# Causal attention on latent heads: score, transposition and weighted-sum products in a new order over eight PSUM banks

## The reference, cut to what matters

```python
q = (_rmsnorm(cq, q_norm) @ w_uq).reshape(B, S, H, MLA_NOPE + MLA_ROPE)
kv = (_rmsnorm(ckv, kv_norm) @ w_ukv).reshape(B, S, H, MLA_NOPE + MLA_V)
...
k = jnp.concatenate([kv[..., :MLA_NOPE], k_rope], axis=-1)
v = kv[..., MLA_NOPE:]
o = _dense_causal_attention(q * (MLA_NOPE + MLA_ROPE) ** -0.5, k, v)
return o @ w_out
```

## Time and profile before

| what | value |
|---|---|
| median of three runs | 4548.55 us (4546.48 to 4549.56) |
| the profiled execution | 4549.86 us |
| its span in the profile | 4548.1 us |
| TensorE busy, whole span | 94% |
| the mla stage, first score to first product of mla_out | 2483.86 to 2652.44 us |
| granted TensorE clock, mean of the stage | 0.86 of full |

### The profile page before, as it was taken

The page is one execution under the profiler, slowest core; times in us unless marked ns, Lnnn a source line. Parts: engine busy times, 40 slices in busy tenths (PEclk is TensorE's granted clock), DMA queues, the critical chain, the costliest instruction groups (busy, mean ns, idle before and its releaser), DMA issues.

```text
span 4548.1 us, 40760 instructions
## 1 busy us (share of the span) xinstructions
PE 4278.2 (94%) x15992; PEld 2741.9 (60%) x15992; DVE 1575.2 (35%) x2912; ACT 685.8 (15%) x1462; POOL 1670.0 (37%) x1520
## 2 busy tenths in 40 slices
PE   7948999999999999999999789999999889989998
PEld 3324444444644444488863348888888436847887
DVE  3062111026711110333225633324432754453432
ACT  1131000012610000100012420001000231211000
POOL 0002988800049887044410004443444015003442
PEclk9969999999899999899999889999999889989999
DMA  3103434321034342122221012222222123102222
GB/s 122 65 0 111 157 143 157 117 72 56 10 134 157 143 157 102 60 88 88 86 71 43 1 47 88 88 86 77 88 81 90 52 80 99 36 28 84 84 88 70
DMA packets 124350, 387.45 MB, mean 85 GB/s; under 512 B 37568, under 2 KB 40640, under 8 KB 110080
## 3 DMA queue, kind: packets, MB, share of 16 engines
q1 hardware_dynamic: 108848, 302.56, 20.0%
q0 software_dynamic: 15312, 82.28, 4.7%
HBM read 376.40 MB, written 8.39 MB: 85 GB/s over the span
## 4 chain that ended last, share of the span: by engine, by line
PE 90%; DVE 6%; ACT 2%; issue 1%; DMA 0%; POOL 0%; DVEq 0%; POOLq 0%; ACTq 0%
PE bank L723 89%; ACT temporary L1340 1%; DVE temporary L2370 1%; DVE small_columns L2158 1%; DVE temporary L2155 1%; ACT normed L1340 0%; ACT area_b L1340 0%; DVE normed L1740 0%; DMA vector_columns<-in_vectors_dram 0%; DVE temporary L1898 0%; DVE area_b L1861 0%; DVE temporary L1974 0%; DVE small_columns L1978 0%; DVE temporary L1902 0%; PE bank L1002 0%
## 5 line engine op out<-in xcount | busy, mean ns | idle before, releaser
L723 PE MATMUL bank<-normed,weight_ring 128*128 128x512 f32 (+2 forms) x4080 | 1508.9, 527 | 17.4 <-DVE normed L1746 5.8
L723 PEld LDWEIGHTS bank<-normed,weight_ring 128*128 128x128 f32 (+1 forms) x4080 | 779.6, 192 | 698.1 <-issue 636.8
L723 PE MATMUL bank<-area_a,weight_ring 128*128 128x512 f32 (+1 forms) x1776 | 636.4, 515 | 8.2 <-issue 8.2
L723 PEld LDWEIGHTS bank<-area_a,weight_ring 128*128 128x128 f32 x1776 | 339.3, 192 | 282.0 <-issue 259.7
L723 PE MATMUL bank<-area_b,weight_ring 128*128 128x256 f32 (+3 forms) x1616 | 501.9, 458 | 5.8 <-issue 2.8
L673 POOL TENSOR_TENSOR area_b<-weight_ring 128x512 f32<-128x512 f32 (+1 forms) x68 | 84.2, 1239 | 1141.3 <-issue 569.7
L643 POOL TENSOR_SCALAR area_b<-area_b,small_columns 128x384 f32<-128x384 f32 x336 | 417.8, 1243 | 0.0
L723 PEld LDWEIGHTS bank<-area_b,weight_ring 128*128 128x128 f32 (+2 forms) x1616 | 303.7, 188 | 179.7 <-issue 148.7
L645 POOL TENSOR_TENSOR area_b<-area_b 128x384 f32<-128x384 f32 x336 | 334.4, 995 | 28.0
L723 PE MATMUL bank<-area_b 128*128 128x256 f32 (+2 forms) x1200 | 258.6, 378 | 16.2 <-ACT area_d L1340 16.2
L673 POOL TENSOR_TENSOR area_d<-weight_ring 128x512 f32<-128x512 f32 (+1 forms) x68 | 84.2, 1239 | 446.6 <-PE bank L723 422.2
(11 more groups left out here) (277 smaller groups left out, 4535.8 us busy)
## 6 DMA issues: line engine op xcount, KB each, us to landing
weight_ring<-in_weights_dram SPq DMA_DIRECT2D x377, 512.0 KB, 4.6
weight_ring<-in_weights_dram SPq DMA_DIRECT2D x61, 1024.0 KB, 4.8
area_b<-in_weights_dram POOLq DMA_DIRECT2D x48, 1024.0 KB, 5.4
area_b<-in_weights_dram POOLq DMA_DIRECT2D x48, 512.0 KB, 6.6
weight_ring<-in_weights_dram SPq DMA_DIRECT2D x40, 384.0 KB, 4.3
weight_ring<-in_weights_dram SPq DMA_DIRECT2D x24, 256.0 KB, 3.8
low_scratch<-area_d SPq DMA_DIRECT2D x16, 256.0 KB, 2.0
area_d<-low_scratch SPq DMA_DIRECT2D x16, 256.0 KB, 2.8
```

The lines of the kernel that those rows point to most:

```text
L723: i = pe.matmul(out, lhsT, rhs, start=start, stop=stop)
```

## The change

Only the stage "mla" changes; the number of units, heads and blocks stays.

1. **Banks.** Scores get banks 4 to 7 by unit, turned blocks banks 0 and 1 by unit, outputs banks 2 and 3 by head. The table `MLA_ORDER` goes; each kind of result has its own semaphores.
2. **Outputs one block at a time.** The four output products of a head are no longer issued together. Product b of head hd is issued in the turn of unit 4·hd + b + 8 (`MLA_OUT = 8`), between that unit's score and the turned blocks of the unit three before. Each head's first one waits until ACT has copied the head's four units.
3. **Scale and mask.** DVE adds the mask only to the unit's own 128 columns (the diagonal block), in place in the bank, and takes the maximum straight from the bank. The scale goes into the exponential (`scale=`) and into the negation of the maximum. ACT's exponential reads the bank and writes `TM`.
4. **1/sum.** DVE no longer multiplies the probabilities by 1/sum. It writes a 128x128 diagonal matrix of 1/sum (`ts(mla_diagonal(v), const("ident"), ...)`), four of them in turn in the last row of `D` ("area_d").
5. **Transposition as a product.** In place of a transposition TensorE does a float32 product of the unnormalised block with the diagonal matrix, which transposes and normalises at once: two passes of 128 columns in place of one.
6. **ACT's order.** exp(u), then (every fourth unit, from the third head on) the store of the head three behind, then copy(u-2).

```diff
-stage("mla", 0, 16 * 9, 0)
+stage("mla", 0, 0, 0)
...
+        MLAG, MLA_OUT = 3, 8
+
+        def mla_scores(u):
+            return bank[4 + u % 4]
+
+        def mla_diagonal(u):
+            return D[:, 9, u % 4 * P:(u % 4 + 1) * P]
+
+        def mla_turned(u):
+            return bank[u % 2]
+
+        def mla_output(hd):
+            return bank[2 + hd % 2]
...
-            for u in range(16 * NB + MLAG):
+            for u in range(16 * NB + MLA_OUT):
                 if u < 16 * NB:
                     hd, n = u // NB, u % NB
-                    s = small()
-                    mm(sbank(s)[:, 0:(n + 1) * P], A[0:96, hd, n * P:(n + 1) * P], B[0:96, hd, 0:(n + 1) * P], True, True,
-                       small_full)
-                if u >= MLAG:
+                    if u >= 4:
+                        pe.wait_ge(S("mla_exp"), u - 3)
+                    mm(mla_scores(u)[:, 0:(n + 1) * P], A[0:96, hd, n * P:(n + 1) * P], B[0:96, hd, 0:(n + 1) * P],
+                       True, True, S("mla_scored"))
+                if u >= MLA_OUT:
+                    hd, b = (u - MLA_OUT) // NB, (u - MLA_OUT) % NB
+                    if b == 0:
+                        pe.wait_ge(S("mla_copied"), NB * hd + NB)
+                        if hd >= 2:
+                            pe.wait_ge(S("mla_stored"), hd - 1)
+                    rows = slice(64 * (hd % 2), 64 * (hd % 2) + 64)
+                    mm(mla_output(hd)[rows, b * P:], A[:, 16 + 2 * b + hd // 8, hd % 8 * 64:hd % 8 * 64 + 64],
+                       B[:, 16 + 4 * (hd % 2) + b, b * P:], b == 0, b == NB - 1,
+                       S("mla_summed") if b == NB - 1 else None)
+                if 0 <= u - MLAG < 16 * NB:
                     v = u - MLAG
-                    hd, n = v // NB, v % NB
-                    s = small()
+                    n = v % NB
                     pe.wait_ge(S("mla_probs"), v + 1)
+                    if v >= 2:
+                        pe.wait_ge(S("mla_copied"), v - 1)
                     for b in range(n + 1):
-                        i = pe.transpose(sbank(s)[:, b * P:(b + 1) * P], TM[:, v % 4, b * P:(b + 1) * P], const("ident"))
-                    i.then_inc(small_full, 1)
-                    if n == NB - 1:
-                        o = small()
...
+                        mm(mla_turned(v)[:, b * P:(b + 1) * P], TM[:, v % 4, b * P:(b + 1) * P], mla_diagonal(v), True, True,
+                           S("mla_transposed") if b == n else None)
...
-                    p = TM[:, o, 0:(n + 1) * P]
-                    a(p, p, ACT.Exp, bias=SM[:, o:o + 1], accum_out=SM[:, 4 + o:5 + o]).then_inc(S("mla_exp"), 1)
...
+                    a(TM[:, o, 0:(n + 1) * P], mla_scores(u)[:, 0:(n + 1) * P], ACT.Exp, scale=scale, bias=SM[:, o:o + 1],
+                      accum_out=SM[:, 4 + o:5 + o]).then_inc(S("mla_exp"), 1)
...
-                    stook(stt(w, sbank(s)[:, 0:(n + 1) * P], scale, C[:, CAT["causal"] + 512 - (n + 1) * P:CAT["causal"] + 512],
-                              ALU.mult, ALU.add), s)
-                    sdone(dve, s)
+                    w, own_keys = mla_scores(u)[:, 0:(n + 1) * P], mla_scores(u)[:, n * P:(n + 1) * P]
+                    dve.wait_ge(S("mla_scored"), u + 1)
+                    own(tt(own_keys, own_keys, C[:, CAT["causal"] + 384:CAT["causal"] + 512], ALU.add))
                     own(dve.tensor_reduce(SM[:, o:o + 1], w, AX, ALU.max))
...
-                    ts(w, w, SM[:, 8 + o:9 + o], None, ALU.mult).then_inc(S("mla_probs"), 1)
+                    if v >= 4:
+                        dve.wait_ge(S("mla_transposed"), v - 3)
+                    ts(mla_diagonal(v), const("ident"), SM[:, 8 + o:9 + o], None, ALU.mult).then_inc(S("mla_probs"), 1)
```

More of the change, by code:

```diff
@@ L1094, in _ @@
             begin("mla_out")
-            sdone(pe, mla_small("output", 14))
-            sdone(pe, mla_small("output", 15))
+            pe.wait_ge(S("mla_stored"), 16)
             for j in range(DB):
@@ L1574, in _, with stored @@
                 took(a(B[0:64, j, :], pbank(m0 + j)[0:64, :], ACT.Identity), m0 + j)
-            for u in range(16 * NB + MLAG - 1):
+            scale = float(96 ** -0.5)
+            def stored(hd):
+                rows = slice(64 * (hd % 2), 64 * (hd % 2) + 64)
+                act.wait_ge(S("mla_summed"), hd + 1)
+                a(H[rows, hd // 2, :], mla_output(hd)[rows, :], ACT.Identity).then_inc(S("mla_stored"), 1)
+            for u in range(16 * NB + MLA_OUT):
                 if u < 16 * NB:
@@ L1577, in _ @@
                     n, o = u % NB, u % 4
+                    if u >= 4:
+                        act.wait_ge(S("mla_transposed"), u - 3)
                     act.wait_ge(S("mla_minus_max"), u + 1)
[L1579 to L1582 removed]
+                    a(TM[:, o, 0:(n + 1) * P], mla_scores(u)[:, 0:(n + 1) * P], ACT.Exp, scale=scale, bias=SM[:, o:o + 1],
+                      accum_out=SM[:, 4 + o:5 + o]).then_inc(S("mla_exp"), 1)
@@ L1583, in _ @@
+                if u >= MLA_OUT + NB and u % NB == 0:
+                    stored(u // NB - 3)
                 v = u - MLAG + 1
-                hd, n = v // NB, v % NB
-                s = mla_small("turned", v)
-                sfull(act, s)
-                if v >= 8 and n == 0:
-                    sfull(act, mla_small("output", hd - 2))
-                stook(a(B[:, 16 + 4 * (hd % 2):17 + 4 * (hd % 2) + n, n * P:(n + 1) * P],
-                        sbank(s)[:, 0:(n + 1) * P].rearrange("p (b t) -> p b t", t=P), ACT.Identity), s)
@@ L1591, in _ @@
-                if n == NB - 1:
-                    s = mla_small("output", hd)
-                    rows = slice(64 * (hd % 2), 64 * (hd % 2) + 64)
-                    sfull(act, s)
-                    stook(a(H[rows, hd // 2, :], sbank(s)[rows, :], ACT.Identity), s)
+                if 0 <= v < 16 * NB:
+                    hd, n = v // NB, v % NB
+                    act.wait_ge(S("mla_transposed"), v + 1)
+                    if v >= 8 and n == 0:
+                        act.wait_ge(S("mla_summed"), hd - 1)
+                    a(B[:, 16 + 4 * (hd % 2):17 + 4 * (hd % 2) + n, n * P:(n + 1) * P],
+                      mla_turned(v)[:, 0:(n + 1) * P].rearrange("p (b t) -> p b t", t=P), ACT.Identity)\
+                        .then_inc(S("mla_copied"), 1)
@@ L1596, in _ @@
+            stored(15)
             norm(8)
@@ L2150, in _ @@
                     n, o = u % NB, u % 4
[L2151 to L2157 removed]
+                    w, own_keys = mla_scores(u)[:, 0:(n + 1) * P], mla_scores(u)[:, n * P:(n + 1) * P]
+                    dve.wait_ge(S("mla_scored"), u + 1)
+                    own(tt(own_keys, own_keys, C[:, CAT["causal"] + 384:CAT["causal"] + 512], ALU.add))
                     own(dve.tensor_reduce(SM[:, o:o + 1], w, AX, ALU.max))
[L2159 removed]
+                    ts(SM[:, o:o + 1], SM[:, o:o + 1], -scale, None, ALU.mult).then_inc(S("mla_minus_max"), 1)
                 if u >= 1:
```

19 lines of the change are left out of this document (removed).

## The result

| | before | after |
|---|---|---|
| median | 4548.74 us (4 runs) | 4508.38 us (4505.63 to 4512.0, 4 runs) |
| profiled execution | 4549.86 us | 4505.63 us |
| span | 4548.1 us | 4503.8 us |
| stage, first score to first product of mla_out | 168.6 us | 128.5 us |
| one head in the steady state, clock at 1.00 | 9.09 us | 7.91 us |

The ratio is 0.9913, with a 95% interval of 0.9895 to 0.9930: 40 us faster, where 54.8 were forecast. The stage is 40.1 us shorter, and that is all of the median's difference. At full clock 16 heads give 16·(9.09 − 7.91) = 18.9 us of it; the other 21.2 is time that the kernel before spent at the lower clock, less a difference at the ends. The profiled execution is 4 us better still: its stage starts 2.9 us earlier than before, behind the same instructions.

A forecast was written before the change was run, and what follows sets the result against it. Before, DVE's work and the output products between a score and its user set the head's length; after, TensorE bounds it: 16·6.9 + 3.4 = 113.8 us against 168.6, 54.8 less, so 4494 us, range 4484 to 4515.

The forecast's parts named there:

- A: Stage mla: the clock keeps falling, mean 0.86, a head takes 8.0 us and the kernel 4512 us; chance 15%.
- B: Stage mla: ACT's strict order stalls TensorE once a head, 1.2 us, 19 us in all, kernel 4513 us; chance 8%.
- TensorE's waits behind the output products go: Stage mla: DVE's wait of 2.60 us a head loses its cause; TensorE's own waits are small and at the ends.
- TensorE becomes the bound: Stage mla: TensorE at 6.9 us a head exceeds DVE's 5.3 and ACT's 4.7, so it sets the pace.
- DVE's total, 5.3 us a head: DVE in stage mla: 6.49 us less 0.81 for scale and mask and 0.40 for normalisation, at most 5.7.
- The clock: Stage mla: mean granted clock 0.97 or more after the change, against 0.86 before.
- C: Stage mla: the clock falls to 0.50 and stays, a head takes 13.8 us, kernel slower at 4604 us; chance 4%.
- The diagonal product, 1.3 us a head dearer: TensorE in stage mla: 2.54 us a head for diagonal products against 1.2 for transpositions, 21 us in all.
- TensorE's total, 6.9 us a head: TensorE in stage mla: scores 2.14, outputs 2.14, diagonal products 2.54 and 0.1 more, at full clock.
- A diagonal pass, 0.127 us: TensorE's turned blocks: each pass takes 0.127 us, from eight such passes in 1.16 us; 20 passes a head.
- The ends, 3.4 us: Start and end of stage mla: 1.9 us lost in the first eight units, 0.65 for the last copy, 0.85 for the store.
- The cause: Stage mla: spreading the output products, at most one before a score in its unit, removes DVE's 2.60 us wait a head.

## Why the prediction was right, and where it was off

Time, sign and range held: 4508 within 4484 to 4515, but 14 us above the 4494 of the forecast, so a quarter of the forecast gain was missing. The forecast's own band (a head between 6.6 and 7.4 us, 4489 to 4502) was missed. That 4508 lies in the range at all is luck: the range reached up to 4515 to take in the rivals A (4512) and B (4513), neither of which occurred; what came in their place was a cost of 1.36 us a head that the prediction had at 0.1.

- *TensorE's waits behind the output products go.* Right, by the waits.
- *TensorE becomes the bound.* Right: 99% occupied, 1.6 us of waits.
- *DVE's total, 5.3 us a head.* Right: 73.8 of 110 us, 5.3 of 7.91. So it was nowhere near deciding.
- *The clock.* Right: 1.00, and with it the 20 us that the forecast gave to the lower clock less the ends (21.2 measured); of the 35 us for the head at full clock only 18.9 came. Rivals A and C didn't occur, nor B: TensorE waited for ACT 0.3 us in all.
- *The diagonal product, 1.3 us a head dearer.* Right in size (7.91 − 6.60 = 1.31), by the run that undid it, but with luck: ten passes are 1.1 of it, and 0.2 is the dearer step back from 64 columns, which the prediction didn't know. Its passes at 0.127 in place of 0.11 made up for that.
- *TensorE's total, 6.9 us a head.* **This step failed**, at the term "0.1 because ten passes that should take 7·0.43 + 0.27 = 3.28 took 3.39 to 3.41". That 0.11 to 0.13 was read from a piece in which only one group followed another, output products and then a score; it is the price of one step from 64 to 128 columns (the same piece takes 3.25 with 128 columns throughout), and I entered it as one for the head. The changed order has four steps to 64 and four back. Measured: 6.55 without them, and 1.36 for them. The 6.9 held 0.35 too much, nearly all of it the diagonal passes (20·(0.127 − 0.11) = 0.34), and lacked the 1.36: 6.9 − 0.35 + 1.36 = 7.91.
- *A diagonal pass, 0.127 us.* Measured: 0.11. The group of eight that it was read from the earlier trace rows stands right behind passes with 64 columns. A little earlier in the same trace the same kind of group stands behind passes with 128 columns and takes 1.05 us, not 1.16. The 0.11 between them is what the turned blocks lose here too (0.33 against 0.22); the prediction spread it over seven passes.

```profile
3824.67 1.05 PE L723 MATMUL bank<-temporary,area_d 128*128 128x128 f32 x8
...
3826.51 0.67 PE L723 MATMUL bank<-area_d,temporary 64*64 64x64 f32 x8
```

- *The ends, 3.4 us.* 128.5 − 16·7.91 = 1.9. Too dear by 1.5, which offset a little.
- *The cause.* The prediction put the gain down to the spreading ("no score has more than one output product before it"). The runs show that it was the distance; the spreading itself cost 14.6 us with outputs of 64 columns and nothing with 128. In the order before, TensorE waits for the last turned block's copy with the next score behind that wait, and DVE's wait of 2.60 us is for that score. With the score's user and the output's source both far away, a piece of 2.1 us between two scores harms nobody: it makes no head longer in the three runs that have it eight units behind.

What stays open: why the clock fell in the kernel before. The three kernels in which TensorE waits 1.46 to 1.49 us for a copy once a head had 0.84 to 0.88 in the stage; all others had 1.00, the one with the output products in one piece eight units behind too, where TensorE waits for ACT 3.7 us in 15 short waits and for DVE 3.1 in 4, of 100 us. No run varied these waits in steps.

## What to carry to other kernels

Put a product that needs a copy made by another engine far enough behind in TensorE's order that the copy is long done. Where its weights have another number of columns than their neighbours, issue it whole: in four pieces it cost 14.6 us more here; with the same number it made no difference. Where TensorE sets the pace, keep the number of weight columns the same between groups of short products, even if half of the result is thrown away (20 us here; in the kernel before, where TensorE waits, nothing that can be told), and count every change as a term of its own in a sum. Moving work from an engine that is busy 83% to the one that sets the pace costs what it costs there: here 160 transpositions made into products were 20 us.

## What the runs showed of the hardware that was not expected

Going from passes with 128 columns of weights to passes with 64 and back costs 0.33 to 0.34 us at 2.4 GHz, over and above the passes: 7.91 against 6.55 us a head with four such changes, 6.88 with one. The way back alone costs 0.14 in front of a score (3.39 against 3.25 for ten passes). With 128 columns throughout, the next load starts 0.11 us ahead of its pass, hidden. The depth in rows, 96 or 128, makes no difference (stage 128.5 us both times), nor do 256 more waits on semaphores already past their value (128.7). A float32 transposition is one pass of 0.11 us, a float32 product of the same size two.
